# RWKV-7 and Conformer layers with expert routing on one core: norms in groups of two tiles, router logits with the router's columns stationary

## The chip, the core and the metric

The kernel runs on one core of a Trainium2 chip. The metric is the device time of one execution in microseconds. The core has TensorE (PE; its weight loads are listed as PEld), VectorE (DVE), ScalarE (ACT), GpSimd (POOL) and SyncE (SP, which here only issues DMA), and 16 DMA engines.

## What is computed

The input is 512 tokens of width 1024, float32. Two layers each add a token mixer and a mixture of experts to the residual `h`; a last RMS norm gives the output. Layer 0 mixes with RWKV-7, layer 1 with a Conformer convolution module of width 31.

```python
def rms_norm(x, g):
    y = x * rsqrt(mean(x * x, axis=-1) + 1e-6)
    return y * g

for i in range(2):
    hn = rms_norm(h, norm1_g[i])
    h = h + (rwkv7_time_mix(hn) if i == 0 else conformer_conv(hn))
    hn = rms_norm(h, norm2_g[i])
    h = h + hierarchical_moe(hn)
return rms_norm(h, final_g)

def hierarchical_moe(ht):
    gp = softmax(ht @ w_group + b_group)          # 4 groups
    p_top, g = top_k(gp, 1)
    el = (ht @ w_expert + b_expert)[its group g]  # 8 experts each
    top_l, e = top_k(el, 2)
    gates = softmax(top_l) * p_top
    return sum over the 2 chosen: gate * (silu(ht @ w_gate[e]) * (ht @ w_up[e])) @ w_down[e]
```

The router's logits are therefore 36 columns (4 groups and 32 experts) for each token.

## The kernel before

The tokens stand in four tiles of 128 (TT = 4, P = 128), a tile's tokens on the partitions; `h` is [128, 4, 1024]. A norm has three parts. ScalarE squares a tile and sums it (`act_norm_rows`, L394; in front of the experts L491). The factor is worked out by VectorE (`ss/D + eps`, L440 or L528) and by ScalarE as exp(-0.5 ln) (L398, L400; L496, L498). VectorE writes the normalised rows `hn` (L430; in front of the experts L526, without the factor). TensorE then transposes each tile in eight 128x128 pieces (`pe_norm_columns`, L452) into PSUM, and ScalarE copies them, in two halves, to `hnT` (L410, L503), which is what products read.

Three norms (`act_norm` and `dve_norm`) go by groups of tiles, whose factors are worked out together: the first norm, in front of RWKV, takes all four tiles as one group (ALL_TILES); the convolution's norm and the final norm take tiles 0 to 2, then tile 3 (LAST_ALONE). In front of these two, VectorE also adds the experts' results into `h` (`dve_combine`, L889, two instructions a tile), in order of tiles, and ScalarE squares a tile once this is done. There are only two `hn` buffers in the first and the convolution's norm, so tile 2 is written when tile 0 has been transposed.

The first norm's scale vector `g_row` (L1066) and the blend factors `mu` (L1067) count on one semaphore, `params_in`, and VectorE waits for both before it writes rows (L426).

After a mixer, `pe_mix_out` projects its output tile by tile (L1689), VectorE adds it to `h` (`dve_mix`, L1720), and the norm in front of the experts follows tile by tile. At the end stands `pe_route_last`: transposes of tile 2, logits of tiles 0 and 1, transposes of tile 3, logits of tiles 2 and 3. A tile's logits (`pe_logits`, L471) are eight products that accumulate; each has a 128x128 piece of `hnT` as stationary weights and streams the router's 36 columns:

```python
for c in range(C):
    last = nc.tensor.matmul(bank[LOGIT_BANKS[t]][:, t * N_LOGITS:(t + 1) * N_LOGITS],
                            m.hnT[:, c, t * P:(t + 1) * P], m.w_route[:, c, :], ...)
```

Then `dve_route` scales the logits with the tile's factor (L546), three tiles at once and the last by itself, and finds groups, experts and slots. `pe_ranks` first issues five idle products of 512 columns (`pe_stay_busy`, L626) and then counts the ranks (L634 to L638) once VectorE has the picks. POOL (`pool_moe`) scales the rows (L698) and stores them to DRAM (L700), clears two buffers (L703), and gathers the rows of a pair of experts (L717) once VectorE has the gather table (L671). `pe_moe` runs the 32 experts. SP loads their weights, 2 MB and 1 MB each, into a ring of six places; the first loads are issued as soon as the last mix projection is done (`mix_ps`), the later ones when a place is free, and places 4 and 5 of the smaller weights when the first gathered rows have landed (`x_in`). In the second half of the routing ScalarE has little to do. After the experts `act_load_back` brings the results back for `dve_combine`.

`pe_conv` begins with the transposes of its norm (L452) and goes on with the products of the first projection (L1921), which read all four tiles. TensorE products in float32 stand as two records each in the trace.

## Time and profile before

| | us |
|---|---|
| median of 3 runs | 1332.46 (1332.44 to 1333.24) |
| the profiled execution, its time | 1331.19 |
| its span in the trace | 1329.5 |
| TensorE busy | 1173.6 (88%) |
| VectorE busy | 531.3 (40%) |
| ScalarE busy | 380.2 (29%) |
| POOL busy | 239.9 (18%) |
| mean rate of DMA | 204 GB/s |

The span runs from the first to the last instruction of the trace; the device time of the same execution is 1.7 us longer. Times in the rows count from the span's start. RWKV fills the span to some 541 us, its routing to 571, the experts of layer 0 to 801, the convolution to 1042, its routing to 1071, the experts of layer 1 to 1301, and the final norm the rest.

### The profile page before, as it was taken

The numbers are of one execution on the slowest core, as the hardware profiler recorded it, in microseconds if no ns is written. First come the engines' busy times: TensorE is split into PE (matmuls) and PEld (weight loads), VectorE is DVE, ScalarE is ACT, GpSimd is POOL, SyncE is SP. The second block draws the span as 40 slices with busy tenths as digits, with TensorE's granted clock in tenths as the row PEclk, the third lists the DMA queues.
The fourth block names the chain that finished last, engine by engine and source line by source line (L and its number), as shares of the span: only waits on it lengthen the run. The fifth ranks groups of instructions, "written<-read, shape, count | busy, mean of one in ns | idle before, by whom it ended". The sixth has DMA issues, their size and how long they took to land.

```text
span 1329.5 us, 27899 instructions
## 1 busy us (share of the span) xinstructions
PE 1173.6 (88%) x11900; PEld 639.5 (48%) x11900; DVE 531.3 (40%) x942; ACT 380.2 (29%) x729; POOL 239.9 (18%) x243
## 2 busy tenths in 40 slices
PE   4999999999999889989988882999999999987880
PEld 2365655555556544645544441444434655544440
DVE  6845544554545423411111114489962321111114
ACT  3333333433343222111111113356641111111112
POOL 2000000000000001322221110388810422221110
PEclk9999999999999899799999996999999899999896
DMA  5011010110100243789999996215400689999985
GB/s 163 3 54 38 22 49 23 35 38 22 50 28 30 100 189 123 306 321 425 425 423 426 425 394 258 87 63 228 168 21 0 253 318 423 425 424 426 426 336 213
DMA packets 50202, 271.85 MB, mean 204 GB/s; under 512 B 16386, under 2 KB 19586, under 8 KB 31648
## 3 DMA queue, kind: packets, MB, share of 16 engines
q1 hardware_dynamic: 38048, 240.67, 44.9%
q0 software_dynamic: 10880, 21.00, 4.2%
q10 hardware_dynamic: 1152, 8.39, 1.6%
q8 instruction: 96, 1.57, 0.5%
q14 instruction: 26, 0.21, 0.0%
HBM read 263.73 MB, written 23.07 MB: 216 GB/s over the span
## 4 chain that ended last, share of the span: by engine, by line
PE 60%; DMA 20%; DVE 10%; POOL 3%; ACT 3%; issue 2%; SPq 1%; POOLq 0%; DVEq 0%; ACTq 0%
DMA big<-in_moe_w_gate_up_dram 18%; PE psum L1214 13%; PE psum L785 9%; PE psum L1689 8%; PE psum L1403 5%; PE psum L798 4%; POOL big L1896 3%; DVE psum L2031 3%; PE psum L1393 3%; PE psum L1921 2%; DVE h L889 2%; PE psum L471 2%; PE psum L764 1%; PE psum L1351 1%; PE psum L1489 1%
## 5 line engine op out<-in xcount | busy, mean ns | idle before, releaser
L785 PE MATMUL psum<-big 128*64 128x256 f32 x1728 | 217.8, 396 | 42.4 <-DMA big<-in_moe_w_gate_up_dram 30.7
L1214 PE MATMUL psum<-big 128*128 128x512 f32 x384 | 192.5, 619 | 5.0 <-ACT big L1252 5.0
L785 PEld LDWEIGHTS psum<-big 128*64 128x64 f32 x1728 | 120.7, 141 | 124.9 <-DMA big<-in_moe_w_gate_up_dram 42.4
L860 DVE TENSOR_TENSOR big<-big,psum 128x128 f32<-128x128 f32 x64 | 18.4, 288 | 322.6 <-ACT big L826 322.6
L698 POOL TENSOR_SCALAR big<-big 128x1024 f32<-128x1024 f32 x8 | 22.8, 2848 | 595.3 <-PE psum L452 595.2
L726 POOL DMA_INDIRECT chosen<-big x64 | 63.7, 996 | 346.6 <-ACT big L836 183.8
L798 PE MATMUL psum<-big 128*64 128x512 f32 x512 | 120.8, 592 | 1.2 <-ACT big L831 1.2
L1689 PE MATMUL psum<-big 128*128 128x512 f32 x256 | 114.9, 601 | 0.6 <-ACT big L2001 0.6
L1921 PE MATMUL psum<-big,conv_w 128*128 128x512 f32 x256 | 110.4, 593 | 2.2 <-ACT big L410 1.2
L1896 POOL TENSOR_TENSOR big<-big 128x512 f32<-128x512 f32 x81 | 103.0, 1271 | 43.6 <-ACT big L1982 33.1
L1545 ACT COPY big<-psum 128x512 f32<-128x512 f32 x96 | 57.3, 623 | 138.2 <-PE psum L1403 74.7
L1214 PEld LDWEIGHTS psum<-big 128*128 128x128 f32 x384 | 64.7, 189 | 57.3 <-issue 49.8
L2031 DVE SCALAR_TENSOR_TENSOR psum<-big,conv_taps,psum 128x512 f32<-128x512 f32 x125 | 83.0, 751 | 0.0
L1403 PEld LDWEIGHTS psum<-big 64*64 64x64 f32 x3072 | 62.2, 135 | 39.4 <-issue 39.3
L1921 PEld LDWEIGHTS psum<-big,conv_w 128*128 128x128 f32 x256 | 48.5, 190 | 63.4 <-issue 62.1
L1689 PEld LDWEIGHTS psum<-big 128*128 128x128 f32 x256 | 47.6, 191 | 56.6 <-issue 53.0
L1403 PE MATMUL psum<-big 64*64 64x64 f32 (+1 forms) x3072 | 70.4, 231 | 3.3 <-issue 2.0
L1982 ACT ACTIVATE big<-big,conv_taps 128x512 f32<-128x512 f32 x89 | 60.4, 716 | 40.3 <-DVE big L2014 21.2
L831 ACT COPY big<-psum 128x128 f32<-128x128 f32 x64 | 17.1, 267 | 174.6 <-PE psum L771 174.6
L836 ACT COPY big<-psum 128x512 f32<-128x512 f32 x64 | 37.5, 587 | 93.1 <-PE psum L798 93.1
L798 PEld LDWEIGHTS psum<-big 128*64 128x64 f32 x512 | 36.6, 137 | 47.0 <-issue 36.5
L452 PE MATMUL psum<-ident,big 128*128 128x128 f32 x128 | 20.9, 328 | 36.8 <-DVE big L430 35.2
(252 smaller groups left out, 1402.7 us busy)
## 6 DMA issues: line engine op xcount, KB each, us to landing
big<-in_moe_w_gate_up_dram SPq DMA_DIRECT2D x54, 2048.0 KB, 27.6
big<-in_moe_w_down_dram SPq DMA_DIRECT2D x64, 1024.0 KB, 33.0
conv_w<-in_moe_w_gate_up_dram SPq DMA_DIRECT2D x10, 2048.0 KB, 32.5
big<-in_rwkv_w_rkv_dram SPq DMA_DIRECT2D x24, 512.0 KB, 3.2
conv_w<-in_conv_w_pw_dram SPq DMA_DIRECT2D x8, 1024.0 KB, 4.9
big<-chosen ACTq DMA_DIRECT2D x8, 1024.0 KB, 7.9
big<-in_rwkv_w_o_dram SPq DMA_DIRECT2D x4, 1024.0 KB, 4.9
rows<-big POOLq DMA_DIRECT2D x8, 512.0 KB, 6.3
```

What stands on the lines that cost most here:

```text
L726: nc.gpsimd.indirect_dma_start(chosen[m.layer], bass.IndirectOffsetOnAxis(ap=m.scatter_at[:, e:e + 1].bitcast(u32), axis=0), m.y[e % Y_RIN ...
L785: last = nc.tensor.matmul(o[half * SLOTS:(half + 1) * SLOTS, 0:F_EXP].rearrange("p (u f) -> p u f", u=2), m.xT[e // 2 % 2][:, c, (e % 2) * ...
L798: last = nc.tensor.matmul(bank[6 + e % 2][half * SLOTS:(half + 1) * SLOTS, :], m.zT[e % 2][:, k, :], m.down[j][:, k, half * 512:(half + 1) ...
L1214: last = nc.tensor.matmul(bank[b], m.w[:, n, c, :], x[:, c, :], start=(c == 0), stop=(c == C - 1))
L1393: last = nc.tensor.matmul(bank[b][half(par), at:at + CH], lhs(hd, cp, par), rhs(hd, cp, par), start=True, stop=True)
L1403: last = nc.tensor.matmul(bank[b + hd][half(par ^ (hd & crossed)), at:at + w.shape[1]], lhs(hd, cp, par), w, start=True, stop=True)
L1545: nc.scalar.copy(dst, src).then_inc(done.now(), 1)
L1689: return nc.tensor.matmul(bank[4 * (t % 2) + nh], src[:, c, t * P:(t + 1) * P], wts[:, nh * 512:(nh + 1) * 512], start=(c == 0), stop=(c = ...
L1896: nc.gpsimd.tensor_tensor(out_, m.product[n % 4], m.product[(n - 1) % 4] if k == 1 else out_, ALU.add).then_inc(m.pool_tap, 1)
L1921: last = nc.tensor.matmul(bank[2 + 2 * b + u], m.w1[b][:, c, u, :], m.hnT[:, c, :], start=(c == 0), stop=(c == C - 1))
L1982: nc.scalar.activation(m.product[n % 4], m.u[b][:, at:at + T], ACT.Copy, scale=m.taps[:, q, at:at + 1]).then_inc(m.product_ready, 1)
L2031: nc.vector.scalar_tensor_tensor(out=acc[k % 2], in0=m.u[b][:, k:k + T], scalar=w[:, k:k + 1], in1=acc[k % 2], op0=ALU.mult, op1=ALU.add). ...
```

## The change

Four things change.

- The groups of all three grouped norms become tiles 0 and 1, then 2 and 3 (TWO_AND_TWO). In `dve_norm` a group's factors are now worked out once the first tile of the next group is ready, and its rows are written once all tiles of the next group are.
- The logits of tiles 0 to 2 have the router's 36 columns as stationary weights and stream the 128 tokens; they come out transposed, 36 x 128. ScalarE copies them to `logitsT`, TensorE turns them back with one transpose a tile (`pe_flip_logits`), and the last tile is done as before (`pe_last_logits`).
- `pe_conv` begins with eight idle products of 512 columns, which wait for the combination of tile 0.
- `mu` has a semaphore of its own. Semaphores are shared elsewhere (ranks on that of the logits, the clearing of the gather's buffers on that of the scaling).

```diff
-        LAST_ALONE = ((0, TT - 1), (TT - 1, TT))
-        ALL_TILES = ((0, TT),)
-        NORM_GROUPS = (ALL_TILES, EACH_TILE, LAST_ALONE, EACH_TILE, LAST_ALONE)
+        TWO_AND_TWO = ((0, TT // 2), (TT // 2, TT))
+        NORM_GROUPS = (TWO_AND_TWO, EACH_TILE, TWO_AND_TWO, EACH_TILE, TWO_AND_TWO)
...
+            def factors(g):
+                first, end = groups[g]
+                dve.wait_ge(m.squares.sem, m.squares.by(end))
+                nc.vector.tensor_scalar(m.rstd[:, first:end], m.ss[:, first:end], 1.0 / D, RMS_EPS, ALU.mult,
+                                        ALU.add).then_inc(m.rstd_step.sem, 1)
+
             for g, (first, end) in enumerate(groups):
                 for t in range(first, end):
                     tile_ready(t)
-                if g and groups is LAST_ALONE:
+                    if g and t == first:
+                        factors(g - 1)
+                if g:
                     rows(g - 1)
-                dve.wait_ge(m.squares.sem, m.squares.by(end))
-                nc.vector.tensor_scalar(m.rstd[:, first:end], m.ss[:, first:end], 1.0 / D, RMS_EPS, ALU.mult,
-                                        ALU.add).then_inc(m.rstd_step.sem, 1)
-                if groups is not LAST_ALONE or end == TT:
-                    rows(g)
+            factors(len(groups) - 1)
+            rows(len(groups) - 1)
...
-        LOGIT_BANKS = (0, 0, 0, 1)
+        LOGIT_BANKS = (0, 1, 0)
+        FLIP_BANKS = (4, 4, 4, 5)
...
+            if t >= 2:
+                pe.wait_ge(m.logitsT_ready.sem, m.logitsT_ready.by(t - 1))
             for c in range(C):
-                last = nc.tensor.matmul(bank[LOGIT_BANKS[t]][:, t * N_LOGITS:(t + 1) * N_LOGITS],
+                last = nc.tensor.matmul(bank[LOGIT_BANKS[t]][0:N_LOGITS, 0:P], m.w_route[:, c, :],
+                                        m.hnT[:, c, t * P:(t + 1) * P], start=(c == 0), stop=(c == C - 1))
+            last.then_inc(m.logitsT_in_psum.sem, 1)
+
+        def pe_flip_logits(m, mixer, pe, t):
+            if t == 0:
+                pe.wait_ge(mixer.mixed, TT)
+            pe.wait_ge(m.logitsT_ready.sem, m.logitsT_ready.by(t + 1))
+            nc.tensor.transpose(bank[FLIP_BANKS[t]][:, t * N_LOGITS:(t + 1) * N_LOGITS],
+                                m.logitsT[0:N_LOGITS, t * P:(t + 1) * P],
+                                ident[0:N_LOGITS, 0:N_LOGITS]).then_inc(m.logits_in_psum.sem, 1)
...
+            def logits(t):
+                act.wait_ge(m.logitsT_in_psum.sem, m.logitsT_in_psum.by(t + 1))
+                nc.scalar.copy(m.logitsT[0:N_LOGITS, t * P:(t + 1) * P], bank[LOGIT_BANKS[t]][0:N_LOGITS, 0:P]
+                               ).then_inc(m.logitsT_ready.sem, 1)
...
             square(3)
+            logits(0)
+            logits(1)
             root(3)
             columns(3)
+            logits(2)
...
         def pe_conv(m, pe):
+            pe.wait_ge(moe[0].h_step, 2)
+            for _ in range(8):
+                nc.tensor.matmul(bank[1], ident[:], h[:, 0, 0:512], start=True, stop=True)
             pe_norm(m, pe)
```

TensorE, in front of the experts (both layers), before and with the change. L1689 (L1725) is the last tile's projection, L452 (L458) the transposes, L471 the logits, L626 (L661) the idle products, L634 (L669) the ranks:

```order
L1689 MATMUL psum<-big 128x512 x16
L452 MATMUL psum<-ident,big 128x128 x8
L471 MATMUL psum<-big 128x36 x16
L452 MATMUL psum<-ident,big 128x128 x8
L471 MATMUL psum<-big 128x36 x16
L626 MATMUL psum<-big,ident 128x512 x5
```

```order
L1725 MATMUL psum<-big 128x512 x16
L458 MATMUL psum<-ident,big 128x128 x8
L480 MATMUL psum<-big 36x128 x16
L458 MATMUL psum<-ident,big 128x128 x8
L480 MATMUL psum<-big 36x128 x8
L488 MATMUL psum<-ident,big 128x36 x3
L496 MATMUL psum<-big 128x36 x8
L661 MATMUL psum<-big,ident 128x512 x5
```

The 32 logit products become 24 of the new form, whose output has 36 partitions and 128 columns, then three transposes back (L488), then eight of the old form (L496).

ScalarE at the same place, from the copies of tiles 1 and 2 on; L491 (L518) is a square, L496 and L498 (L523, L525) the root, L503 (L530) the copies to `hnT`, L536 the new copies:

```order
L503 COPY big<-psum 128x4x128 x4
L491 ACTIVATE big<-h 128x1024
L496 ACTIVATE big<-big 128x1
L498 ACTIVATE big<-big 128x1
L503 COPY big<-psum 128x4x128 x2
L620 ACTIVATE big<-big 128x16
```

```order
L530 COPY big<-psum 128x4x128 x4
L518 ACTIVATE big<-h 128x1024
L536 COPY big<-psum 36x128 x2
L523 ACTIVATE big<-big 128x1
L525 ACTIVATE big<-big 128x1
L530 COPY big<-psum 128x4x128 x2
L536 COPY big<-psum 36x128
L655 ACTIVATE big<-big 128x16
```

Two of the new copies stand ahead of tile 3's root, the third is ScalarE's last piece, behind the copies of tile 3.

VectorE, in front of the convolution; L889 (L924) is the combination, two instructions a tile, L440 (L438) the factors, L430 (L431) the rows, L2014 (L2053) the first gate:

```order
L889 SCALAR_TENSOR_TENSOR h<-big,h 128x1024 x6
L440 TENSOR_SCALAR big<-big 128x3
L889 SCALAR_TENSOR_TENSOR h<-big,h 128x1024 x2
L430 SCALAR_TENSOR_TENSOR big<-h,big 128x1024 x3
L440 TENSOR_SCALAR big<-big 128x1
L430 SCALAR_TENSOR_TENSOR big<-h,big 128x1024
L2014 SCALAR_TENSOR_TENSOR big<-psum,conv_vec,big 128x512
```

```order
L924 SCALAR_TENSOR_TENSOR h<-big,h 128x1024 x6
L438 TENSOR_SCALAR big<-big 128x2
L924 SCALAR_TENSOR_TENSOR h<-big,h 128x1024 x2
L431 SCALAR_TENSOR_TENSOR big<-h,big 128x1024 x2
L438 TENSOR_SCALAR big<-big 128x2
L431 SCALAR_TENSOR_TENSOR big<-h,big 128x1024 x2
L2053 SCALAR_TENSOR_TENSOR big<-psum,conv_vec,big 128x512
```

The factors of two tiles instead of three stand at the same place, ahead of the last tile's combination, and two rows instead of one follow the last factors.

## Rows read from the trace of the kernel before

**Rows 1.** The page, part 4: the chain that ended last, by line.

```profile
DMA big<-in_moe_w_gate_up_dram 18%; PE psum L1214 13%; PE psum L785 9%; PE psum L1689 8%; PE psum L1403 5%; PE psum L798 4%; POOL big L1896 3%; DVE psum L2031 3%; PE psum L1393 3%; PE psum L1921 2%; DVE h L889 2%; PE psum L471 2%; PE psum L764 1%; PE psum L1351 1%; PE psum L1489 1%
```

**Rows 2.** Timeline, first norm (start us, us, engine line op, [idle before <-releaser]).

```profile
7.81 1.03 ACT L394 ACTIVATE psum<-h 128x1024 f32<-128x1024 f32 x1 [0.71 <-DMA h<-in_x_dram]
...
12.49 4.78 PE L452 MATMUL psum<-ident,big 128*128 128x128 f32 x24 [12.49 <-DVE big L430]
...
16.25 1.29 DVE L430 SCALAR_TENSOR_TENSOR big<-h,big 128x1024 f32<-128x1024 f32 x1 [0.42 <-PE psum L452]
```

**Rows 3.** The norm's scale vector: its transfer, issued from line 1066.

```profile
L1066 SPq DMA_DIRECT2D big<-in_norm_g_dram x1: 738/738/738, 2.7 to 2.7; - x1
...
DMA to landing us min/median/max: 6.9/6.9/6.9
```

**Rows 4.** Timeline, layer 0, from the router's first product to the gather.

```profile
541.87 3.66 PE L471 MATMUL psum<-big 128*128 128x36 f32 x32
...
546.99 6.88 PE L471 MATMUL psum<-big 128*128 128x36 f32 x32
547.23 1.07 ACT L503 COPY big<-psum 128x512 f32<-128x512 f32 x2 [2.29 <-PE psum L452]
...
553.90 0.26 DVE L546 SCALAR_TENSOR_TENSOR big<-psum,big 128x36 f32<-128x36 f32 x1 [2.73 <-PE psum L471]
...
566.41 1.09 POOL L717 DMA_INDIRECT big<-rows,big  x1 [13.04 <-DVE big L674]
```

**Rows 5.** Windows: us, busy us of each engine, granted clock, DMA share, GB/s.

```profile
120.00:430.00 310.00, 296.74 (x5845) 177.35 (x5846) 157.97 (x246) 119.62 (x206) 0.00 (x0) 1.00 0.11 35
...
546.00:548.00 2.00, 2.00 (x12) 2.00 (x10) 0.00 (x0) 0.77 (x2) 0.23 (x1) 0.50 0.99 418
...
565.00:566.00 1.00, 1.00 (x4) 0.48 (x3) 0.85 (x6) 0.00 (x0) 0.00 (x0) 1.00 0.41 164
...
600.00:631.00 31.00, 31.00 (x228) 16.89 (x224) 5.31 (x11) 5.46 (x15) 7.39 (x9) 1.00 1.02 427
...
822.00:824.00 2.00, 1.69 (x8) 1.72 (x9) 1.45 (x2) 0.03 (x1) 0.00 (x0) 0.50 0.79 246
...
826.00:828.00 2.00, 0.59 (x5) 0.62 (x6) 1.28 (x1) 1.97 (x6) 0.00 (x0) 1.00 1.03 424
```

**Rows 6.** Timeline, layer 1: router's first products, last tile's scaling, gather.

```profile
1043.35 3.66 PE L471 MATMUL psum<-big 128*128 128x36 f32 x32
...
1055.13 0.25 DVE L546 SCALAR_TENSOR_TENSOR big<-psum,big 128x36 f32<-128x36 f32 x1 [2.73 <-PE psum L471]
...
1066.79 1.08 POOL L717 DMA_INDIRECT big<-rows,big  x1 [12.60 <-DVE big L674]
```

**Rows 7.** Row transfers: first gather in the chain; all gathers; all stores.

```profile
566.41 4.31 DMA big<-rows,big
...
DMA to landing us min/median/max: 3.5/10.7/12.5
...
DMA to landing us min/median/max: 3.0/6.3/10.4
```

**Rows 8.** Timeline, the convolution's norm.

```profile
818.17 0.17 DVE L440 TENSOR_SCALAR big<-big 128x3 f32<-128x3 f32 x1 [1.29 <-ACT psum L394]
...
820.88 2.61 DVE L430 SCALAR_TENSOR_TENSOR big<-h,big 128x1024 f32<-128x1024 f32 x2
...
826.34 1.28 DVE L430 SCALAR_TENSOR_TENSOR big<-h,big 128x1024 f32<-128x1024 f32 x1 [0.50 <-ACT big L400]
...
827.41 2.09 PE L452 MATMUL psum<-ident,big 128*128 128x128 f32 x16 [1.63 <-ACT big L410]
...
830.68 14.86 PE L1921 MATMUL psum<-big,conv_w 128*128 128x512 f32 x34 [1.18 <-ACT big L410]
```

**Rows 9.** Timeline, the final norm's last tile.

```profile
1324.52 0.15 DVE L440 TENSOR_SCALAR big<-big 128x1 f32<-128x1 f32 x1
...
1325.18 1.28 DVE L430 SCALAR_TENSOR_TENSOR big<-h,big 128x1024 f32<-128x1024 f32 x1 [0.51 <-ACT big L400]
```

More of the change, by code:

```diff
@@ L173, in bass_hybrid_rwkv7_conformer_hmoe @@
         moe_rows_stored = sem("moe_rows_stored")
+        moe_logitsT_in_psum = sem("moe_logitsT_in_psum")
+        moe_logitsT_ready = sem("moe_logitsT_ready")
         moe_logits_in_psum = sem("moe_logits_in_psum")
@@ L237, in __init__ @@
                 self.idx = m.take(N_EXP)
+                self.logitsT = m.take((TT - 1) * P)
                 self.scatter_at = m.take(N_EXP)
@@ L469, in pe_logits, with pe_last_logits @@
                 pe.wait_ge(mixer.mixed, TT - 1)
+            if t >= 2:
+                pe.wait_ge(m.logitsT_ready.sem, m.logitsT_ready.by(t - 1))
             for c in range(C):
-                last = nc.tensor.matmul(bank[LOGIT_BANKS[t]][:, t * N_LOGITS:(t + 1) * N_LOGITS],
+                last = nc.tensor.matmul(bank[LOGIT_BANKS[t]][0:N_LOGITS, 0:P], m.w_route[:, c, :],
[8 more added lines that the diff above has]
+                                ident[0:N_LOGITS, 0:N_LOGITS]).then_inc(m.logits_in_psum.sem, 1)
+        def pe_last_logits(m, pe):
+            t = TT - 1
+            pe.wait_ge(m.hnT_ready.sem, m.hnT_ready.by(2 * TT))
+            for c in range(C):
+                last = nc.tensor.matmul(bank[FLIP_BANKS[t]][:, t * N_LOGITS:(t + 1) * N_LOGITS],
                                         m.hnT[:, c, t * P:(t + 1) * P], m.w_route[:, c, :], start=(c == 0),
@@ L482, in pe_route_last @@
             pe_logits(m, mixer, pe, 2)
-            pe_logits(m, mixer, pe, TT - 1)
+            for t in range(TT - 1):
+                pe_flip_logits(m, mixer, pe, t)
+            pe_last_logits(m, pe)
         def act_moe_norm(m, mixer, act):
@@ L545, in dve_route @@
                     dve.wait_ge(m.logits_in_psum.sem, m.logits_in_psum.by(TT - 1 if t == 0 else TT))
-                last = nc.vector.scalar_tensor_tensor(out=m.logits[:, t, :], in0=bank[LOGIT_BANKS[t]][:, t * n:(t + 1) * n],
+                last = nc.vector.scalar_tensor_tensor(out=m.logits[:, t, :], in0=bank[FLIP_BANKS[t]][:, t * n:(t + 1) * n],
                                                       scalar=m.rstd[:, t:t + 1], in1=m.b_route, op0=ALU.mult, op1=ALU.add)
@@ L640, in pe_ranks @@
                                         stop=(t == TT - 2), skip_group_check=True)
-            last.then_inc(m.rank_in_psum.sem, 1)
+            last.then_inc(m.logits_in_psum.sem, 1)
             pe_stay_busy(m, 1)
@@ L991, in __init__ @@
                     "mixed").split())
+                self.mu_in = sem("rwkv_mu_in")
                 self.wo_in = [sem(f"rwkv_wo_in{j}") for j in range(PAIRS // 2)]
@@ L2148, in _ @@
                     act_conv(cv, act, tile_ready)
-            for g in range(len(LAST_ALONE)):
-                act_norm_rows(fin, act, tile_ready, LAST_ALONE, g)
+            for g in range(len(TWO_AND_TWO)):
+                act_norm_rows(fin, act, tile_ready, TWO_AND_TWO, g)
         @block.vector
```

31 lines of the change are left out of this document (15 added, 16 removed).

## Prediction

> **What bounds the kernel now.** I read the chain of waits first, for what is worth shortening. Its largest single item is the transfer of expert weights [rows 1], and in the weight stage the DMA engines are full at 427 GB/s, as from 600 to 631 us [rows 5]. A stage that starts earlier therefore ends earlier by the same time, but nothing inside it gets shorter. Both routings bear this out: from the landing of the first gathered rows (566.41 + 4.31 = 570.72 us) [rows 7] the stage's length is set by bytes. What the change can save lies in front of the two weight stages and behind the second: the norm at the start, the logits twice, the convolution's norm, and the final norm. I took the timeline of each for who ends last, and the windows for TensorE's granted clock (1.00 is 2.4 GHz, 0.50 is 1.2).
>
> **1. First norm.** VectorE computes all four factors once all four squares are there; the fourth normalised row is written at 16.25 + 1.29 = 17.54 [rows 2]. VectorE's differences and blends follow at once and the first products wait for those, so this 17.54 is what counts. Now tiles 0 and 1 have their own factors. Tile 2 has arrived at 7.81 [rows 2]; the factors need it only because they stand behind that wait on VectorE. Factor and root take 0.66 together (from 1324.52 to 1325.18 [rows 9]), and VectorE can start them at 8.0: ready by 8.75. The rows also wait for the scale vector, which lands at 2.67 + 6.9 = 9.6 [rows 3]; that ends last. Since `mu` now has a semaphore of its own, the rows no longer wait for it. Rows 0 and 1: 9.65 + 2 x 1.28 = 12.2. TensorE then binds: 24 transposes took 4.78 us, and the row at 16.25 was released by the sixteenth [rows 2], so 16 took 3.7 from 12.49: I take 1.95 for the first eight and 1.8 for the next. From 11.1 these end at 13.05 and 14.9; row 3 waits for the second: 14.95 + 1.29 = 16.25. **Gain 1.3**, bounds 0.5 (vector later) and 2.1 (eight transposes in 1.05 us [rows 8]). ScalarE does squares 2 and 3 (1.22 each) behind the first root, ready by 11.2; nobody waits for them.
>
> **2. Logits, layer 0.** Before: 32 records (a product stands as two) of 36 columns in 3.66 us from 541.87, so 0.109 each; then eight transposes; then 32 more from 546.99 to 553.87, 0.215 each, the granted clock being 0.50 [rows 4, 5]. VectorE takes the last tile at 553.90. The new form loads 36 columns as weights and streams 128. At full clock 34 records of 512 columns take 14.86 us [rows 8], 0.437 each; a quarter is 0.109, so at full clock both forms cost the same 0.11. **The whole gain is the clock.** It fell to 1.2 GHz behind the first 32 products of 36 columns [rows 4, 5]. Between 120 and 430 us, where the recurrence's many 64-column products have their share, it stood at 1.00 [rows 5]. I take 2.4 GHz throughout. Then: first 16 products end 545.4, transposes of the last tile 1.05: 546.4, tile 2's products 1.75: 548.15. ScalarE copies them to 548.5 (0.3, my estimate for 128 columns from 0.53 for 512 [rows 4]); flips 0 and 1 are done meanwhile, flip 2 costs 0.15 more. ScalarE's order is square 3, logits 0 and 1, root 3, columns 3, logits 2: the copies of columns 3 (1.07 for two [rows 4]) run 546.5 to 547.6, before they are wanted. Last products 548.6 + 1.75 = 550.35, against 553.87: **3.5**. VectorE's scaling of tiles 0 to 2 (three of 0.26 or less [rows 4]) hides under them; were it not hidden it would cost 0.8.
> From there to the gather: 566.41 - 553.90 = 12.5 in layer 0, 1066.79 - 1055.13 = 11.7 in layer 1 [rows 4, 6]. In layer 0 the five idle products (ten records of 0.85 at half clock) delayed the ranks. I credit **0.55** of the 0.85.
> POOL: its last scaling starts 546.5 instead of 547.8, the store is issued 549.4, and with a store's longest 10.4 us [rows 7] it lands 559.8, before the gather's new time of 562.3. It stays hidden; a landing later than 12.9 us would bind.
> New collision: the loads of weights issued at 541 run into 565 to 566, 0.41 full [rows 5]. The gather, due 4.05 earlier at 562.3, now meets their last 3 us. Alone it took 4.31, with the stream full 10.7 in the middle [rows 7]: over 2.5 us it advances at 0.4 of its pace, **loss 1.0** (bounds 0 and 2.5). Layer 0: 3.5 + 0.55 - 1.0 = **3.1**.
>
> **3. Convolution's norm.** Before: after combine 2, done 816.88, VectorE idles 1.29 for its squares, combine 3 ends 820.85, rows 0 and 1 take 2.61, row 2 waits for TensorE, factors of the last tile, row 3 ends 827.62; TensorE waits for ScalarE, transposes from 827.41, first product 830.68 [rows 8]. Now: combine 2 ends 816.9, factors of 0 and 1 to 817.1 (squares long there), combine 3 to 819.75, rows 0, 1 to 822.4, factors 822.55, roots to 823.3 (VectorE idles 0.75), rows 2 and 3 to 825.9, eight transposes 826.95, two copies 828.05. **Gain 2.6.** The idle products (8 x 2 records) start at combine 0's end, 811.65 (816.88 less two combinations of 2.62). At half clock all would take 13.7 and end 825.3; the clock came back within 4 us of TensorE's start there, between 822 and 826 [rows 5]. Eight products at full clock take 7.0, and each slow microsecond adds half: with 3 to 6 slow they end 820.2 to 821.7, at most 0.6 after row 0 is written at 821.05. TensorE has slack until row 2 (824.6), which hides that. Bounds 1.0 and 2.7.
> The row: in 822 to 824 the clock stands at 0.50, TensorE does 16 transposes and nothing else, and in 826 to 828 it stands at 1.00 [rows 5, 8]. By that, transposes keep the clock. The Trainium skill ("TensorE: Matmul & The Clock Gate", Part 4: PE-mode transpose) says that transpose mode does not count as busy for the clock gate. By that rule the eight transposes of tile 3 would run at half clock after the idle products' end and cost 0.9 more; the trace disagrees.
>
> **4. Logits, layer 1.** Same sum: 1043.35 + 3.5 + 1.05 + 1.75 + 0.5 + 1.75 = 1051.9, against 1055.13 [rows 6]: **3.2**. The ranks were not late here. Its first loads are 6 MB where layer 0's are 8, so at 427 GB/s they end 4.9 us sooner after the projection, near 1062; the gather comes at 1063.6: no loss.
>
> **5. Final norm.** The same 1.29 gap goes, and one root's 0.65 with only row 3 behind it becomes one with two rows behind it. Combine 3 ends 1319.4, rows 0, 1 1322.0, factors and root to 1322.95, rows 2, 3 to 1325.55, against 1325.18 + 1.28 = 1326.46 [rows 9]: **0.9**. The four output stores stay 1.3 apart.
>
> Merged semaphores, the zeroing signal and the new tile cost nothing: they add no wait.
>
> **Sum.** 1.3 + 3.1 + 2.6 + 3.2 + 0.9 = 11.1. The profiled execution took 1331.19 (span 1329.5): 1320.1. The median, 1332.46, is 1.27 above it: **1321.4**.
>
> **Rivals.**
> *A, the clock falls all the same* (the new weights still fill only 36 columns of the array). For it: nothing in the trace has 36 columns as weights. Against: 64-column weights held it for the whole weight stage. Then both routings keep 0.215 per record and add the copy, flips and a wait: +1.0 each. 1332.46 - 1.3 - 2.6 - 0.9 + 2.0 = 1329.7. Chance 0.11, half of it on either side of the bound of 0.2%.
> *B, transposes don't keep the clock* (the skill's rule above). Worked from rows: eight at half clock 1.95 instead of 1.05: 1322.3. Chance 0.05.
> *C, the routing's gain is swallowed in the weight stage*, because the ring's first loads set the stage's end. Against it: DMA has idle time before the gather in both layers. 1332.46 - 1.3 - 2.6 - 0.9 = 1327.7. Chance 0.03.
> *D, slower: the gathers now meet the weight loads.* Without any loss at the gathers the sum is 12.1. If each takes the longest loaded time, 12.5 instead of 4.3 [rows 7], the two lose 16.4: 1332.46 - 12.1 + 16.4 = 1336.8. It decides from a landing of 10.3 us on. Against it: the loads end 3 us into layer 0's gather and before layer 1's. Chance 0.03.
>
> **How the numbers follow.** The forecast has 0.78. Its range: all upper bounds give 13.5, hence 1319, and a clock that happens to fall elsewhere, as all of TensorE's later work is shifted, may give one more: 1318. The lower bounds (0.5, 1.5, 1.0, 2.5, 0.6) give 6.1: 1326.4; with B and a little of C, 1327. What can be told from no change is 0.2%, 2.7 us. Faster: 0.78 + B + C + half of A = 0.92; same 0.05; slower 0.03.
>
> **What would show it.** Granted clock 1.00 from 541 to 553 and 1043 to 1055 (shifted); the last logits' products ending some 8.5 us after the first begin; VectorE's first difference starting at 16.3 (17.57 before); first product of the convolution 2.6 us sooner after the load back; TensorE at 1.00 when its transposes start. Wrong if the clock stands at 0.50 there, if the gather of layer 0 takes over 6 us, or if the weight stage grows by what was saved ahead of it.

## The result, and the profile after

The changed kernel took 1327.31 us (median of 11 runs, 1324.01 to 1331.00), the kernel before 1334.26 (11 runs on the same chips): ratio 0.9945, 95% interval [0.9933, 0.9958], so 7.3 us less, between 5.6 and 8.9. By that ratio the 1332.46 shown ahead becomes 1325.1. The forecast was 1321.4, a gain of 11.1 us, with a range of 1318 to 1327: the direction held, the time lies in the range, and the gain came out a third smaller than forecast. Timed a second time (experiment after_again) the ratio was 0.9931 [0.9911, 0.9950]. Two executions of the experiments below lie far outside all others, 1736.47 us in groups_clear (mean granted clock 0.649) and 3978.09 in warm_only (1.000), and medians and ratios leave them out.

Both kernels were profiled twice, the second time in the experiments below. The program is cut here at rows that both have, and each number is the time from one cut to the next. "Last blend" is the start of VectorE's addition of the last tile's mixer output to `h` (L1720 before, L1756 after), the last scaled logits are at L546 (L581), the first gather at L717 (L752). The landing is the start of the loads that wait for it (L350, L351), and the load behind the first expert is the first one at L345 (L346) after that. The load back is at L881 (L916). Unlike the single trace that I predicted from, two profiles show which segments repeat and which don't.

| segment (us) | before, two profiles | after, two profiles | difference of means | forecast |
|---|---|---|---|---|
| start to end of the first norm's last row | 17.54 / 16.79 | 17.36 / 16.95 | 0.0 | -1.3 |
| to the last blend of layer 0's recurrent stage | 523.66 / 523.93 | 525.17 / 524.02 | +0.8 | 0 |
| last blend to last tile's scaled logits, layer 0 | 12.70 / 12.84 | 9.95 / 9.94 | -2.8 | -3.5 |
| to the first gather | 12.51 / 12.34 | 13.26 / 13.26 | +0.8 | -0.55 |
| gather to its landing | 4.32 / 4.42 | 4.48 / 4.21 | 0.0 | +1.0 |
| landing to the first load behind the first expert | 7.86 / 9.42 | 6.53 / 6.53 | -2.1 | 0 |
| to the first load back | 225.55 / 225.66 | 225.84 / 225.74 | +0.2 | 0 |
| to the convolution's first product | 26.54 / 27.06 | 24.21 / 24.16 | -2.6 | -2.6 |
| to the last blend of layer 1 | 211.98 / 212.72 | 213.05 / 213.00 | +0.7 | 0 |
| last blend to last scaled logits, layer 1 | 12.47 / 9.17 | 9.95 / 9.95 | -0.9 | -3.2 |
| to the first gather | 11.66 / 13.12 | 12.58 / 12.58 | +0.2 | 0 |
| to the first load behind the first expert | 10.14 / 11.14 | 11.69 / 11.18 | +0.8 | 0 |
| to the first load back | 226.78 / 227.95 | 226.67 / 228.17 | +0.1 | 0 |
| to the end | 25.76 / 25.54 | 24.38 / 24.35 | -1.3 | -0.9 |
| span | 1329.5 / 1332.1 | 1325.1 / 1324.0 | -6.25 | -11.1 |

The chain by line on the page of after (it answers to [rows 1]) is the same chain: weights first, with no new line near the top.

```profile
DMA big<-in_moe_w_gate_up_dram 18%; PE psum L1250 14%; PE psum L820 9%; PE psum L1725 8%; PE psum L1439 5%; PE psum L833 4%; POOL big L1932 4%; PE psum L1429 3%; DVE psum L2070 2%; PE psum L1960 2%; DVE h L924 2%; PE psum L799 1%; PE psum L1525 1%; PE psum L1387 1%; PE psum L1545 1%
```

**First norm.** The chain of waits of after, in order of time (start us, us, what):

```profile
2.67 8.10 DMA big<-in_norm_g_dram
...
10.89 1.29 DVE big L431
...
12.32 3.67 PE psum L458 x16
...
16.08 1.30 DVE big L431
```

The scale vector, not the fourth square, now releases the rows, as the forecast had it. But it took 8.10 us from its issue, where [rows 3] have 6.9, so the rows start at 10.89 and not at 9.65. The 16 transposes took the 3.67 that I had taken from [rows 2]. From the start of the rows to the end of the last one it is 6.48 us, and in [rows 2] it is the same 6.48 (17.54 less the row start at 11.06), so what the new groups can save here is an earlier start of the rows.

**Layer 0's logits.** The timeline of after (start us, us, engine line op, [idle before <-releaser]), answering to [rows 4]:

```profile
542.53 1.23 DVE L1756 TENSOR_TENSOR h<-psum,h 128x1024 f32<-128x1024 f32 x1 [12.21 <-PE psum L1725]
...
543.29 3.68 PE L480 MATMUL psum<-big 128*36 128x128 f32 x32
...
546.91 1.16 PE L458 MATMUL psum<-ident,big 128*128 128x128 f32 x8
...
548.00 1.94 PE L480 MATMUL psum<-big 128*36 128x128 f32 x16
...
549.87 0.67 PE L488 MATMUL psum<-ident,big 36*128 36x36 f32 x3
549.97 0.26 ACT L536 COPY big<-psum 36x128 f32<-36x128 f32 x1 [0.79 <-PE psum L480]
...
550.47 1.98 PE L496 MATMUL psum<-big 128*128 128x36 f32 x16
...
552.38 1.86 POOL L738 MEMSET big<- 128x1024 f32 x2
552.48 0.26 DVE L581 SCALAR_TENSOR_TENSOR big<-psum,big 128x36 f32<-128x36 f32 x1 [1.23 <-PE psum L496]
552.77 1.51 DVE L584 COPY big<-big 128x16 f32<-128x16 f32 x1
```

The windows of after (us, busy us of PE, PEld, DVE, ACT, POOL, granted clock, DMA share, GB/s), answering to [rows 5]:

```profile
541.00:552.00 11.00, 10.89 (x85) 9.34 (x83) 3.85 (x7) 4.16 (x11) 6.49 (x4) 1.00 0.77 291
...
565.00:566.00 1.00, 1.00 (x2) 0.34 (x1) 0.85 (x5) 0.00 (x0) 0.26 (x1) 0.50 0.98 410
...
1040.00:1050.00 10.00, 9.89 (x83) 8.97 (x82) 3.91 (x8) 4.17 (x11) 7.57 (x5) 1.00 0.92 341
```

The clock stood at 1.00 (2.4 GHz) from the last blend to the last scaled logits in both layers, as forecast, and 32 records of the new form took 3.68 us, 0.115 each. Between there and the gather it fell all the same, here in the idle products (0.50 from 565 to 566 us). Two things are not in my sum. Between the transposes' start and the last product's end lie 5.54 us (546.91 to 552.45), where I had 4.95 (545.4 to 550.35): the transposes took 1.09 for 1.00, tile 2's products 1.87 for 1.75, the copy and the flips behind them 0.60 for 0.45, the last products 1.98 for 1.75. And VectorE's copy of 128 x 16 elements took 1.51 us. It ends at 554.28, POOL's two clearings at 554.24. In the kernel before the clearings were over when it came, and it took 0.17 us:

```profile
551.50 1.86 POOL L703 MEMSET big<- 128x1024 f32 x2
...
554.20 0.17 DVE L549 COPY big<-big 128x16 f32<-128x16 f32 x1
```

**Convolution's and final norm.** The timeline of after, answering to [rows 8] and [rows 9]:

```profile
810.54 10.09 PE L1949 MATMUL psum<-h,ident 128*128 128x512 f32 x16 [12.39 <-DVE h L924]
...
818.51 2.61 DVE L431 SCALAR_TENSOR_TENSOR big<-h,big 128x1024 f32<-128x1024 f32 x2
...
821.83 2.60 DVE L431 SCALAR_TENSOR_TENSOR big<-h,big 128x1024 f32<-128x1024 f32 x2 [0.51 <-ACT big L401]
...
824.49 1.15 PE L458 MATMUL psum<-ident,big 128*128 128x128 f32 x8 [0.17 <-DVE big L431]
...
826.80 3.70 PE L1960 MATMUL psum<-big,conv_w 128*128 128x512 f32 x8 [1.16 <-ACT big L411]
...
...
1319.48 2.61 DVE L431 SCALAR_TENSOR_TENSOR big<-h,big 128x1024 f32<-128x1024 f32 x2 [0.51 <-ACT big L401]
```

Both came out as planned: one wait for roots with two rows behind it, and the convolution's first product 24.21 us after the load back. The idle products (16 records from 810.54) ended at 820.63, 0.8 us after row 0 was written (818.51 + 1.3), but row 2 waited for its root and not for TensorE, so that is hidden.

### The profile page after: what moved, and what is told of

The parts are those of the page before. It is cut to its first block, busy times and chain, and to the rows that moved or that the text cites. A ratio compares the mean times of both kernels' runs of the same rounds, so it can differ in the third digit from the quotient of the medians.

```text
span 1325.1 us, 27957 instructions
## 1 busy us (share of the span) xinstructions
PE 1177.8 (89%) x11922; PEld 637.0 (48%) x11922; DVE 533.7 (40%) x943; ACT 381.5 (29%) x737; POOL 240.4 (18%) x243
## 4 chain that ended last, share of the span: by engine, by line
PE 60%; DMA 20%; DVE 10%; POOL 4%; issue 3%; ACT 2%; SPq 1%; POOLq 0%; DVEq 0%; ACTq 0%
DMA big<-in_moe_w_gate_up_dram 18%; PE psum L1250 14%; PE psum L820 9%; PE psum L1725 8%; PE psum L1439 5%; PE psum L833 4%; POOL big L1932 4%; PE psum L1429 3%; DVE psum L2070 2%; PE psum L1960 2%; DVE h L924 2%; PE psum L799 1%; PE psum L1525 1%; PE psum L1387 1%; PE psum L1545 1%
## 5 line engine op out<-in xcount | busy, mean ns | idle before, releaser
L1725 PE MATMUL psum<-big 128*128 128x512 f32 x256 | 114.0, 597 | 0.6 <-ACT big L2040 0.6
L1725 PEld LDWEIGHTS psum<-big 128*128 128x128 f32 x256 | 47.4, 190 | 56.4 <-issue 53.0
L889 DVE COPY big<-psum 128x512 f32<-128x512 f32 x32 | 22.1, 691 | 72.2 <-PE psum L799 72.2
```

The lines of the kernel that those rows point to most:

```text
L1725: return nc.tensor.matmul(bank[4 * (t % 2) + nh], src[:, c, t * P:(t + 1) * P], wts[:, nh * 512:(nh + 1) * 512], start=(c == 0), stop=(c = ...
```

## The experiments

Ratios are to the kernel before on the same chips. The theory to test: the change's worth is the steady clock of the new logits form and the shorter norms, and what is missing was eaten by VectorE's copy and by the vector's landing. The rivals: the logits form is worth nothing, and the clock falls in different places from one execution to the next.

### Parts alone: logits_only, groups_only, no_idle

logits_only keeps the norm groups of before and has no idle products ahead of the convolution; groups_only has the two-and-two groups with the old logits, and no idle products either:

```
-            for t in range(TT - 1):
-                pe_flip_logits(m, mixer, pe, t)
-            pe_last_logits(m, pe)
+            pe_logits(m, mixer, pe, TT - 1)
```

no_idle is the change without

```
-            pe.wait_ge(moe[0].h_step, 2)
-            for _ in range(8):
-                nc.tensor.matmul(bank[1], ident[:], h[:, 0, 0:512], start=True, stop=True)
```

> Of the change only the new form of the logits: groups as before, no idle products ahead of the convolution. Theory (the clock holds under the new form): last tile's scaling 2.6 us sooner after its projection in both layers, granted clock 1.00 there, but VectorE's first copy waits for POOL's clearing (1.1 to 1.5 us instead of 0.17), so the gathers come 1.6 to 2.0 us sooner; time 3.5 us under before. Rival (the gain comes from the groups, the logits gain nothing): within 1 us of before.

> Of the change only the groups of two and two and the semaphore of mu; logits in the old form, no idle products. Theory: first norm's last row 0.2 us sooner, convolution's norm 2.3 us, final norm 1.4 us; routing as before with the clock at 0.50 in it; time 3.5 to 4 us under before. Rival (the idle products carry the convolution's gain): 2 us or less under before, with transposes at half clock on the path.

> The change without its eight idle products. Theory (VectorE's rows set the pace of the convolution's norm, and the clock is back before the last tile's transposes): first product of the convolution at most 0.5 us later than with them, time within 1 us of the change. Rival (they are what the convolution's norm gains by): 1.5 to 2 us slower than the change.

Measured: logits_only 1332.99 us (12 runs), ratio 0.9993 [0.9979, 1.0007]; groups_only 1330.28 (12), 0.9968 [0.9950, 0.9986]; no_idle 1327.99 (6), 0.9949 [0.9930, 0.9968]. Alone, the logits form changed nothing that the timing can tell from zero: 0.9 us, where I expected 3.5, and the interval reaches to 2.8. In its trace the last scaled logits come 9.95 us after the last blend in both layers, as expected. groups_only, which gained the expected 4 us, shows one reason why that is worth less; its timeline of TensorE in layer 0:

```profile
542.70 3.66 PE L477 MATMUL psum<-big 128*128 128x36 f32 x32
546.19 1.12 PE L458 MATMUL psum<-ident,big 128*128 128x128 f32 x8
547.15 3.66 PE L477 MATMUL psum<-big 128*128 128x36 f32 x32
```

The old form's second 32 records took 3.66 us here, not the 6.88 of [rows 4] that I had expected again: its clock did not fall, in either layer (1.00 from 538 to 548 and from 1040 to 1048 us). Last blend to last scaling took 8.82 us, in both layers. The new form took 9.94 to 9.97 in both layers of every trace of it, eight executions in all. So the new form is no faster at full clock. It is 1.1 us slower. The last copy and the flips make 0.60 of that (549.87 to 550.47); the rest is spread over products and transposes, as the first 32 records, which take 3.62 us to the next instruction (543.29 to 546.91) and in the old form 3.49 (542.70 to 546.19). What it buys is that in these traces the time never becomes the 12.5 to 13.1 that the old form takes when its clock falls.

no_idle moves the convolution's first product from 24.21 to 24.56 us behind the load back, within the 0.5 us that I expected; groups_only, also without them, has 24.80. The idle products are worth 0.35 to 0.6 us, less than the timing can tell. Without them TensorE had done nothing for 22.7 us when its first 24 transposes began at 822.32. The windows of no_idle:

```profile
822.00:824.00 2.00, 1.68 (x8) 1.72 (x9) 1.62 (x3) 0.27 (x3) 0.00 (x0) 0.50 0.95 258
824.00:826.00 2.00, 2.00 (x12) 1.85 (x11) 1.38 (x2) 1.41 (x4) 0.00 (x0) 0.63 1.01 403
826.00:828.00 2.00, 1.61 (x14) 1.42 (x13) 1.19 (x1) 1.96 (x4) 0.00 (x0) 1.00 1.01 418
```

Transposes alone brought the clock from 0.50 to 1.00. The rule of the Trainium skill ("TensorE: Matmul & The Clock Gate", Part 4: PE-mode transpose), that transpose mode does not count as busy for the clock gate, is contradicted a second time, after [rows 5].

### The copy beside POOL's clearings: clear_early, groups_clear

```
             for t in range(TT):
+                if t == TT - 1:
+                    pool.wait_ge(m.squares.sem, m.squares.by(TT))
+                    for b in range(2):
+                        nc.gpsimd.memset(m.x[b], 0.0).then_inc(m.scaled.sem, 1)
...
-                pool.wait_ge(m.scaled.sem, m.scaled.by(t + 1))
+                pool.wait_ge(m.scaled.sem, m.scaled.by(t + 1 if t < TT - 1 else TT + 2))
...
-            pool.wait_ge(m.squares.sem, m.squares.by(TT))
-            for b in range(2):
-                nc.gpsimd.memset(m.x[b], 0.0).then_inc(m.scaled.sem, 1)
-            pool.wait_ge(m.scaled.sem, m.scaled.by(TT + 2))
```

groups_clear has the same edit, with the old logits form.

> The change with POOL's two clearings (1.86 us) ahead of its last scaling, when VectorE is idle, instead of behind the last store. Theory (VectorE's copy of 16 columns waits for POOL's clearing, a wait that no semaphore shows): the copy takes 0.17 us again, gathers come 1.35 us (layer 0) and 0.9 us (layer 1) sooner, time 2.3 us under the change. Rival (the copy is slow for another reason, or the later store of the last rows binds the gather): no gain, within 0.5 us of the change.

> The change with POOL's clearing early, but the logits in the old form (36 columns streamed). Theory (the old form loses the clock in some executions and keeps it in others; the new form always keeps it and pays for its copies and flips): from the last projection to the last scaling 8.8 us where the clock holds and 12.5 to 12.7 where it falls, 9.95 for the new form in every trace; so the median is within 2 us of clear_early (1325.6 then), on either side, with more spread. Rival (as predicted: the old form always falls): 12.5 in both layers and 5 us slower than clear_early.

Measured: clear_early 1325.56 us (6 runs), ratio 0.9940 [0.9920, 0.9959]; groups_clear 1328.99 (11), 0.9964 [0.9941, 0.9986]. The timeline of clear_early, POOL, VectorE and TensorE in layer 0:

```profile
544.97 1.86 POOL L734 MEMSET big<- 128x1024 f32 x2
546.79 2.86 POOL L737 TENSOR_SCALAR big<-big 128x1024 f32<-128x1024 f32 x1
...
550.16 0.26 DVE L581 SCALAR_TENSOR_TENSOR big<-psum,big 128x36 f32<-128x36 f32 x1 [1.23 <-PE psum L496]
550.45 0.18 DVE L584 COPY big<-big 128x16 f32<-128x16 f32 x1
...
559.69 5.58 PE L661 MATMUL psum<-big,ident 128*128 128x512 f32 x10
567.09 1.16 PE L799 MATMUL psum<-ident,big 128*128 128x128 f32 x8 [1.83 <-DMA big<-rows,big]
569.81 6.44 PE L820 MATMUL psum<-big 128*64 128x256 f32 x32 [1.55 <-DVE big L890]
```

The copy is back at 0.18 us, in both layers, and the gather follows the scaling by 11.91 us instead of 13.26 in layer 0 and 11.85 instead of 12.58 in layer 1. The copy's wait is thus shown: no semaphore joins the two engines there, and moving the clearings alone removes it. In layer 0 nothing of it reached the weight stage: the gather came 1.35 us sooner after the scaling, landed after 4.91 us instead of 4.48, and the first expert's 32 records took 6.44 us at a clock of 0.55 (570 to 576 us) instead of 3.67. The load behind them was issued 24.3 us after the scaling in after (13.26 + 4.48 + 2.82 + 3.71) and 26.1 us in clear_early (11.91 + 4.91 + 2.83 + 6.48). I had not expected that. The same two rows in after:

```profile
563.33 6.54 PE L661 MATMUL psum<-big,ident 128*128 128x512 f32 x10
...
570.33 1.16 PE L799 MATMUL psum<-ident,big 128*128 128x128 f32 x8 [0.47 <-DMA big<-rows,big]
```

The idle products begin 2.4 us ahead of the gather in both (563.33 and 565.74; 559.69 and 562.07), so they moved with it. But in after the clock fell in them and they took 6.54 us, in clear_early 5.58, and the rows landed 0.43 us later after the gather: 1.83 us of idle time where after has 0.47, and the fall of the clock came in the expert's products. That the earlier copy is the cause isn't shown: logits_only and no_idle, in which the copy waits as in after (1.51 us), had 0.95 and 0.83 us of idle time there and took 5.36 us for the same 32 records. The timing can't tell clear_early from the change, so the 2.3 us that I expected of it can't be confirmed either.

groups_clear was to show whether the old form is the better one once the copy is free. It held its clock in layer 1 (8.82 us) and lost it in layer 0 (13.06), in one execution, as the theory had it; but I expected its time within 2 us of clear_early, and by the ratios it is 3.2 us over it. Three pairs of versions differ in the form alone: groups_only and no_idle (0.9968 and 0.9949) by 2.5 us, groups_clear and clear_early (0.9964 and 0.9940) by 3.2, before and logits_only by 0.9, with intervals that overlap or, in the last pair, one that includes no change at all.

### Steadying the clock otherwise: old_form_idle, clear_warm, warm_only

old_form_idle: the change with the old form and one idle product of 512 columns behind the logits of tiles 0, 1 and 2. clear_warm: clear_early and

```
-            pe_stay_busy(m, 5)
+            pe_stay_busy(m, 6)
...
+                pe.wait_ge(m.y_ready, N_EXP * r + 1)
+                for _ in range(2):
+                    nc.tensor.matmul(bank[6], ident[:], h[:, 0, 0:512], start=True, stop=True)
                 gate_up(0)
```

warm_only: the change with this alone.

> The change with the logits in the old form and one idle product of 512 columns (0.87 us) behind the logits of tiles 0, 1 and 2. Theory (what lies between the narrow products decides about the clock): the clock stays at 1.00 in both layers, from last projection to last scaling 8.8 + 1.7 to 2.6 = 10.5 to 11.4 us. Rival (the narrow products lose the clock whatever lies between them): 0.50 in part of it, over 12.5 us.

> clear_early with six instead of five idle products behind the slots and two between the first transposes and the first expert's products. Theory (the second set of weights is loaded when the first expert's products are done, and these ran at half clock in some executions): from the first expert's first product to that load 3.7 us in both layers instead of 5.4 to 6.5, less up to 0.3 us of delay; time 2 to 3 us under clear_early. Rival (bytes alone set the stage's length, as the prediction said): no gain, 0.3 us slower.

> The change, with idle products only in front of the first expert: six instead of five behind the slots, and two of 512 columns between the transposes of the first gathered rows and the first expert's products. The clearings stay where the change has them. Theory: the first expert's 32 records stand at 3.7 us in both layers (5.4 in layer 1 of the changed kernel, up to 6.6 elsewhere); the 16-column copies still take 1.1 to 1.5 us. Expected ratio 0.9935 to 0.9945, up to 0.9 us under the changed kernel. Rival, the stage's length is set by bytes: the start of the first products makes no difference to the load back, which then comes no earlier than in the changed kernel.

Measured: old_form_idle 1331.36 us (10 runs), 0.9979 [0.9957, 1.0000]; clear_warm 1324.72 (7), 0.9934 [0.9910, 0.9958]; warm_only 1325.96 (6), 0.9943 [0.9925, 0.9961]. TensorE's timeline of old_form_idle in layer 0:

```profile
546.00 1.87 PE L477 MATMUL psum<-big 128*128 128x36 f32 x16
547.71 1.10 PE L482 MATMUL psum<-h,ident 128*128 128x512 f32 x2
548.65 1.87 PE L477 MATMUL psum<-big 128*128 128x36 f32 x16
```

The clock held in both layers, as the theory had it, but the idle products stood in the way: 11.40 us from blend to scaling, against 9.95 of the new form. Turned round, the new form is the cheaper way to hold the clock. In clear_warm it took 3.71 and 3.72 us in the two layers from the first expert's start to the load behind it, as expected; that load came 23.5 us after the scaling in layer 0 (24.3 in after) and 10.6 us after the gather in layer 1 (11.7). Other segments of the same execution were longer: 526.43 us for the recurrent stage, and 229.18 from that load to layer 1's load back. It has the lowest median of all, but not the 2 to 3 us under clear_early that I expected, and its interval holds the change's ratio. warm_only's trace is that of its execution of 3978.09 us (below), so no segment of it is used and its theory of the first expert stays untested there; its ratio agrees with the change's.

### The first norm, all three repairs, and the change once more: vector_early, all_three, after_again

vector_early:

```
             for t in range(TT):
                 sp.dma_start(h[:, t, :], a["x"].rearrange("b (t p) d -> (b t) p d", p=P)[t]).then_inc(h_in[t], 16)
-            sp.dma_start(m.g_row, a["norm1_g"][0:1, :].broadcast_to([P, D])).then_inc(m.params_in, 16)
+                if t == 2:
+                    sp.dma_start(m.g_row, a["norm1_g"][0:1, :].broadcast_to([P, D])).then_inc(m.params_in, 16)
```

> The change, with one DMA moved: SyncE issues the scale vector of the first norm behind the third row tile and ahead of the fourth, not behind the fourth. Theory: the first norm's two early rows wait for that vector (in the changed kernel it landed at 10.77 us, not at the 9.6 of my forecast, and that took 1.1 of the 1.3 us). Then it lands by 10.0, the last row ends at 16.3 to 16.6 instead of 17.36, and the time is 0.5 to 1 us lower, which the timing cannot tell from nothing. Rival: the vector's landing is not set by its place in the queue (128 rows of 4 KB out of one row of DRAM, beside 2 MB of tiles), or the fourth tile now comes later by as much and binds: the last row still ends at 17.0 to 17.5.

> The change with all three repairs: clearings ahead of POOL's last scaling, idle products in front of the first expert, scale vector issued behind the third tile. Theory: against the changed kernel 1.2 to 1.4 us per routing for the copies, up to 1.7 for the first experts, 0.8 for the first norm: 3 to 4 us lower, ratio to the kernel before about 0.992. Rival: the falls of the clock inside the recurrent stage and the taps move by as much and cover it: ratio 0.994 to 0.995 as for the change.

> The changed kernel itself, word for word, timed beside the three variants on the same chip and profiled once more. Expected ratio 0.9945 within 0.0015. If the falls of the clock differ between executions, as they did between two profiles of the kernel before (layer 1's routing 12.47 and 9.17 us, the first expert 5.04 and 6.60), then the recurrent stage (525.17 from the first norm's last row to the last blend) and the first expert's products (3.71 and 5.40) come out otherwise here, while the routing's 9.95 us stands in both layers. Rival: a program's clock falls at the same places each time, then all segments repeat within 0.2 us.

Measured, on one chip: vector_early 1325.93 us (4 runs), 0.9937 [0.9914, 0.9960]; all_three 1325.70 (6), 0.9937 [0.9919, 0.9956]; after_again 1325.07 (6), 0.9931 [0.9911, 0.9950]. The chain of waits of vector_early:

```profile
2.67 7.47 DMA h<-in_x_dram
...
10.17 1.38 DVE big L431
...
15.44 1.30 DVE big L431
```

Now the fourth tile, issued fifth at 2.67 us in the vector's place, lands last and releases the rows. The last row ends at 16.73 (17.36 and 16.95 in the two profiles of the change; 17.25 in all_three, which has the same edit), between what theory and rival had. The rival's mechanism held: in all versions with the new groups the transfer that is issued fifth, vector or tile, ends at 9.8 to 10.8 us (7.09 to 8.10 us after its issue), and exchanging two of them moves the end by less than it varies anyway.

TensorE's timeline of all_three shows what the idle products in front of the first expert cost where the gathered rows come early:

```profile
560.73 5.40 PE L661 MATMUL psum<-big,ident 128*128 128x512 f32 x12
568.13 1.47 PE L799 MATMUL psum<-ident,big 128*128 128x128 f32 x8 [2.01 <-DMA big<-rows,big]
569.40 3.30 PE L842 MATMUL psum<-h,ident 128*128 128x512 f32 x4
572.63 3.67 PE L820 MATMUL psum<-big 128*64 128x256 f32 x32
```

The expert is at full clock again, but starts 4.60 us after the landing instead of 2.82, and the idle products run at half clock in its place. all_three reaches the first load behind the first expert 25.1 us after the scaling, the change 24.3. I had expected a ratio of 0.992 from all_three and got the rival's 0.994. No version is measurably better than the change itself. In the traces each repair of 1 to 2 us stands beside a loss of that size elsewhere; with one execution each, that the one brings the other is not shown.

before_again was the kernel before, profiled a second time:

> The kernel before once more, for one more trace of the same program. Theory (where the clock falls differs from execution to execution): at least one of the two routings or of the two first experts differs by over 1 us from the first trace. Rival (the clock follows the program alone): last projection to last scaling 12.7 and 12.5 us again, first expert 5.0 and 3.7.

It took 1334.16 us. Its timeline in layer 1, the same place as [rows 6]:

```profile
1045.87 3.66 PE L471 MATMUL psum<-big 128*128 128x36 f32 x32
1049.36 1.12 PE L452 MATMUL psum<-ident,big 128*128 128x128 f32 x8
1050.32 3.99 PE L471 MATMUL psum<-big 128*128 128x36 f32 x32
...
1054.35 0.26 DVE L546 SCALAR_TENSOR_TENSOR big<-psum,big 128x36 f32<-128x36 f32 x1 [1.44 <-PE psum L471]
1054.64 1.64 DVE L549 COPY big<-big 128x16 f32<-128x16 f32 x1
```

In the first profile of this same program the last blend to the last scaling took 12.47 us, here 9.17. And here, because the scaling came that early, the copy already met the clearings (1.64 us), in the kernel before. In layer 0 it lost its clock both times (12.70 and 12.84). after_again repeats the change's routing to 0.01 us, while its recurrent stage took 524.02 instead of 525.17 and its layer 1's first expert 3.71 instead of 5.40. So one cause of the lost size is that I had read one execution's clock as the program's.

## Why the prediction was right, and where not

**The first norm (1.3, came 0.0).** The step that failed is "which lands at 2.67 + 6.9 = 9.6". The wait stood as forecast, the size did not: the landing took 8.10 and, in the other profile, 7.69 us (rows from 10.48 on), while the rows of before start at 11.06 and 10.31. Over all profiles but warm_only's, the last row of the eight in which the scale vector is issued fifth under the new groups ends at 16.9 us on the mean, that of the three with one group at 17.2: 0.3 us, less than either varies by. A transfer of one trace was taken as a constant, though the start of the rows in before varies by 0.75 us from run to run. My lower bound of 0.5 had to reach to nothing.

**Layer 0's logits (3.5, came 2.8).** That "at full clock both forms cost the same 0.11" is right to within 0.13 us for 32 records (3.62 against 3.49 to the next instruction). The missing 0.7 is spread: 0.12 in those first records (I had 3.5), and 0.59 behind them, of which the copy and the flips take only 0.15. The ranks' credit of 0.55 was right, 12.43 against 11.91 us in clear_early, but a cost of 1.34 was missing ahead of it: the copy beside the clearings. I had written that the merged signals cost nothing and had asked of POOL only when its store would land, not what would run beside its clearings. The loss of 1.0 at the gather came out as nothing (4.48 and 4.21 us against 4.32 and 4.42), within its bounds of 0 and 2.5.

**The whole gain is the clock.** Half right. The new form held 2.4 GHz in every trace of it. But the old form loses it only sometimes: in layer 0 in both profiles of before and in groups_clear, not in groups_only; in layer 1 in one profile of before (in the other only in its last records), and in neither groups_only nor groups_clear. Hence **layer 1's logits (3.2)** came out at 0.9 on the mean of two profiles: 2.5 against a fallen clock, 0.8 worse than the old form's 9.17. That is the largest error of the sum, below the bound of 2.5 that I gave this term without a row, and rival A's price of 1.0 for the flips was what the form costs whenever the old one would have kept its clock.

**Convolution's norm (2.6, came 2.6) and final norm (0.9, came 1.3).** Both steps held. In the final norm I had 0.95 for factors and roots; from the end of rows 0 and 1 (1316.17 + 2.61) to rows 2 and 3 at 1319.48 they took 0.70. The rest of the 0.4 is within what that segment varies by (25.76 and 25.54 before).

**From the landing of the gather the weight stage's length is set by bytes.** Wrong at its start and right behind it. From the first load behind the first expert to the load back the thirteen traces other than warm_only's agree to about 1% (225.6 to 227.2 us in layer 0, 226.7 to 229.4 in layer 1). In front of that load stands the first expert: from its first record to the load it is 3.71 us at full clock and 5.0 to 6.7 otherwise. "64-column weights held it for the whole weight stage" had overlooked this in the trace that I read, where it is 5.04 us in layer 0 (573.55 to 578.59). The change had 3.71 in layer 0 in both profiles, which gave it 2.1 us that no part of my sum holds; layer 1 gave 0.8 back. As far as the runs show, those 2.1 us are luck: vector_early repeats the 6.53 us from the landing to the load, but no_idle, the same code up to there, has 8.21.

**What the clock took elsewhere.** The recurrent stage and the convolution became longer by 0.8 and 0.7 us. The convolution's part is one place: 20 records at line 1970 took 10.55 us in after, and the same 20 took 8.85 in logits_only; the second profile of before has a fall of the clock there too (0.50 from 958 to 961 us) and 212.72 us. In the recurrent stage it changes from one profile to the next: from 46 to 48 us the clock was 0.50 in after, 1.00 in clear_early and in both profiles of before. My "one more" us for a clock that falls elsewhere was about the right size, but I gave it only to the favourable end.

The rivals: A and D did not happen, nor did B: the transposes of tile 3 took 1.15 us at 824.49. C did in layer 1 alone, where the 0.7 us gained up to the gather met 0.8 lost at the first expert, by its clock and not by the loads. That the time fell in the range rests on errors of both signs, the 2.1 us above against layer 1's missing 2.3. The upper bounds in the text add to 12.95 (2.1 + 4.05 + 2.7 + 3.2 + 0.9), not to 13.5. Adding the differences of the table gives 6.25 us, the timing 7.3 and 9.2; whether the traces or the timings are nearer is left open, as the executions of the change vary by 7 us (1324.01 to 1331.00). That the new form is worth 1 to 3 us on average follows from the three pairs above, whose intervals overlap, and is likely rather than shown.

## What to carry to other kernels

Before a gain is priced from a clock that fell in the trace, profile the kernel twice: a fall that doesn't repeat is worth its price times its frequency, and a form that merely holds the clock must be charged its extra work every time. When a step is moved earlier, list what the other engines do without any semaphore at its new time, GpSimd's writes above all. A number of idle products that reaches to the next work in one execution can fall short in the next, as their own time depends on the clock (4.54 to 6.58 us for the ten records in layer 0 here).

## What the runs showed of the hardware

**A small copy waits for GpSimd.** groups_only shows it at its longest. Its timeline, POOL and VectorE, layer 0:

```profile
551.03 0.59 POOL L706 DMA_DIRECT2D rows<-big  x1 [0.30 <-POOL big L704]
551.14 2.39 DVE L555 COPY big<-big 128x16 f32<-128x16 f32 x1
551.63 1.86 POOL L709 MEMSET big<- 128x1024 f32 x2
```

The copy began before the clearings and ended with them, at 553.53 against 553.49 us. In after the scaling, which reads PSUM beside SBUF, took its usual 0.26 us beside the same clearings at 552.48, and only the copy from SBUF to SBUF waited. The Trainium skill ("SBUF — State Buffer", Who interferes with whom) describes VectorE's second pair of ports as shared with GpSimd and locked for a whole instruction; the trace agrees with a lock that the copy must wait for, and clear_early bears it out. But the copy waited for both clearings, though in after it stood there from 552.77 and the second began at 553.3. The clearings aren't the only ones that hold it: in layer 1 of groups_clear the copy began at 1053.58, beside POOL's scaling of the last rows, which ended at 1053.91, and took 0.36 us, to 1053.94. Here it began during the issue of a store (551.03 to 551.62) and ahead of the clearings; whether that issue held it too, as the times suggest, is open. In clear_warm the copy began at 553.02, 0.1 us before the end of such an issue, and took its 0.17 us, which doesn't decide it.

**One execution in which TensorE was three times slower at a granted clock of 1.00.** The page of warm_only's profiled execution:

```profile
L1253 PE MATMUL psum<-big 128*128 128x512 f32 x384 | 655.6, 1929 | 2.2 <-ACT big L1291 2.2
```

The same 384 products have a mean of 624 ns in after (its line 1250). VectorE's busy time was unchanged (533.8 and 533.7 us). Its cause is open; no other trace shows it.
